# Other orders for the mixer's side steps, norm weights and bias row on VectorE, and a first stage that multiplies two column blocks together

## The reference

```
h = h + 1/2 * SwiGLU_a(RMSNorm(h))                    # d_ff 2816
u = RMSNorm(h) @ W_in                                 # width 3088: GLA q,k,v,gate,low rank; MoBA q,k,v
o = concat(GLA heads (4), MoBA heads (8)) @ W_out
h = h + o
h = h + 1/2 * SwiGLU_b(RMSNorm(h))
h = h + sigmoid(RMSNorm(h) @ W_pg) * (p @ W_pp)
out = RMSNorm(h)
```

## Time and profile before

| | us |
|---|---|
| median of the runs | 524.34 |
| the profiled execution | 523.98 |
| its span (first to last record) | 522.1 |
| TensorE matmul busy | 509.0 |
| VectorE busy | 328.8 |
| ScalarE busy | 277.0 |
| granted TensorE clock, mean | 0.996 |

### The profile page before, as it was taken

One profiled execution on the slowest core, in us unless ns is written; L12 is line 12 of the kernel. 1 busy time (PEld: TensorE's weight loads), 2 busy tenths in 40 slices (PEclk: granted clock), 3 DMA queues, 4 the chain that ended last, 5 costly groups with the idle time before them and its releaser, 6 DMA issues.

```text
span 522.1 us, 6951 instructions
## 1 busy us (share of the span) xinstructions
PE 509.0 (97%) x2499; PEld 413.9 (79%) x2499; DVE 328.8 (63%) x424; ACT 277.0 (53%) x352; POOL 97.0 (19%) x179
## 2 busy tenths in 40 slices
PE   8999999999999999999988999999999999999994
PEld 5778888888788888887776788888888888888883
DVE  4686556665636465699774885655656555473675
ACT  4974454444535276855674675345453452542836
POOL 1404232223210110220331000223222232120000
PEclk9999999999999999999999999999999999999998
DMA  8999888786787865754689385778778768648202
GB/s 255 369 312 340 269 245 254 210 243 214 237 262 266 263 219 207 241 163 125 211 281 249 126 298 171 256 243 257 222 229 255 236 229 240 219 136 273 75 0 80
DMA packets 79991, 117.20 MB, mean 224 GB/s; under 512 B 5952, under 2 KB 51984, under 8 KB 79840
## 3 DMA queue, kind: packets, MB, share of 16 engines
q1 hardware_dynamic: 71472, 93.34, 57.1%
q0 software_dynamic: 8336, 23.49, 13.4%
q10 hardware_dynamic: 160, 0.07, 0.0%
HBM read 106.12 MB, written 12.33 MB: 227 GB/s over the span
## 4 chain that ended last, share of the span: by engine, by line
PE 83%; DMA 5%; DVE 3%; ACT 3%; issue 2%; SPq 2%; POOL 1%; DVEq 0%; ACTq 0%; POOLq 0%
PE acc L568 81%; DMA pr_dram<-pr_sq 3%; SPq L431 1%; DMA prT<-pr_dram 1%; PE side L568 1%; DMA raw<-in_ffn_w_gu 1%; DVE w_lo L1243 1%; POOL prT L517 1%; PE turn L608 1%; ACT junk L938 1%; DVE gg L1530 0%; ACT w_hi L927 0%; PE turn L568 0%; DVE pr_sq L1507 0%; DVE AT L1553 0%
## 5 line engine op out<-in xcount | busy, mean ns | idle before, releaser
L1243 DVE TENSOR_TENSOR w_lo<-raw,w_hi 128x2048 fp32r<-128x2048 f32 (+1 forms) x87 | 192.6, 2216 | 98.1 <-ACT w_hi L927 97.9
L927 ACT ACTIVATE w_hi<-raw 128x2048 fp32r<-128x2048 f32 (+1 forms) x87 | 161.0, 1856 | 103.8 <-PE acc L568 103.7
L568 PE MATMUL acc<-w_hi,hT_hi 128*128 128x512 f32 x496 | 195.2, 393 | 0.5 <-DVE w_lo L1243 0.2
L568 PE MATMUL acc<-w_hi,hT_lo 128*128 128x512 f32 x496 | 193.2, 389 | 0.0
L568 PE MATMUL acc<-w_lo,hT_hi 128*128 128x512 f32 x496 | 193.1, 389 | 0.0
L568 PEld LDWEIGHTS acc<-w_hi,hT_hi 128*128 128x128 f32 x496 | 93.1, 188 | 22.0 <-issue 1.2
L568 PEld LDWEIGHTS acc<-w_hi,hT_lo 128*128 128x128 f32 x496 | 93.1, 188 | 19.7
L568 PEld LDWEIGHTS acc<-w_lo,hT_hi 128*128 128x128 f32 x496 | 93.2, 188 | 18.9
L479 POOL DMA_DIRECT2D act_in<-act_dram x92 | 50.1, 551 | 119.8 <-DMA act_dram<-act_sq 112.7
L568 PE MATMUL acc<-w_hi,a_hiT 128*128 128x512 f32 x176 | 68.6, 390 | 0.0
L568 PE MATMUL acc<-w_lo,a_hiT 128*128 128x512 f32 x176 | 68.5, 389 | 0.0
(11 more groups left out here) (178 smaller groups left out, 324.3 us busy)
## 6 DMA issues: line engine op xcount, KB each, us to landing
raw<-in_ffn_w_gu SPq DMA_DIRECT2D x82, 512.0 KB, 5.0
raw<-in_ffn_w_down SPq DMA_DIRECT2D x40, 512.0 KB, 5.3
raw<-in_w_in SPq DMA_DIRECT2D x24, 512.0 KB, 4.6
act_dram<-act_sq POOLq DMA_DIRECT2D x23, 256.0 KB, 5.5
act_in<-act_dram POOLq DMA_DIRECT2D x92, 64.0 KB, 3.6
raw<-in_w_out SPq DMA_DIRECT2D x8, 512.0 KB, 5.3
raw<-in_w_ple_gate SPq DMA_DIRECT2D x8, 512.0 KB, 5.5
raw<-in_ffn_w_gu SPq DMA_DIRECT2D x10, 256.0 KB, 6.1
```

The costliest lines, as they stand in the source:

```text
L568: return nc.tensor.matmul(o, lhsT, rhs, start=start, stop=stop, skip_group_check=True)
L927: A(w_hi[:, slot, :nk * N], raw[:, slot, :nk * N], ACT.Copy).then_inc(hi_ready, 1)
L1243: V.tensor_tensor(w_lo[:, slot, :nk * N], raw[:, slot, :nk * N], w_hi[:, slot, :nk * N].bitcast(F32), ALU.subtract).then_inc(lo_ready, 1)
```

## The change

1. First stage. The first four units become chunk pairs: unit u holds chunks 2u and 2u+1 of blocks 0 and 1 side by side. TensorE computes both blocks chunk by chunk (`first_pair`), so 12 matmuls per chunk of x, and for units 2 and 3 block 0 ahead of block 1. The pieces are five; units 2 and 3 are loaded and split whole. The order of ScalarE and VectorE: chunk 0 of x, pieces 0 and 1, chunk 1, piece 2, chunks 2 and 3, pieces 3 and 4, chunks 4 to 7, unit 2, then the squares, the root, unit 3. The first Silu comes behind the splits of units 4 and 5. The table loaded at the start is that of Sqrt instead of Silu.
2. Norm weights and bias row. TensorE's two steps go; `small_rows` does both on VectorE with two 32x32-square transposes, four copies, a memset and nine copies of bucket values. GpSimd sets two small tiles to zero and issues two DMAs less.
3. Mixer. `MIX`, `ACT_STEPS` and `DVE_STEPS` are reordered; no step is added or removed.

```diff
 MIX = {
     (35, 0): ["lr"],
     (35, 1): ["z"],
-    (37, 0): ["T_a"],
-    (38, 3): ["lv0"],
-    (40, 1): ["T_k0", "T_k1", "lv1"],
-    (40, 3): ["sc0.0", "sc0.1"],
-    (41, 0): ["lv2"],
-    (41, 2): ["sc1.0", "sc1.1"],
-    (42, 2): ["sc2.0", "sc2.1", "lv3"],
-    (43, 2): ["sc3.0", "sc3.1", "pv0"],
-    (44, 3): ["pv1"],
-    (45, 1): ["pvg0"],
-    (45, 3): ["pvg1", "pv2"],
+    (38, 0): ["T_a"],
+    (40, 1): ["T_k0", "T_k1"],
+    (40, 3): ["sc0.0", "sc0.1", "lv0"],
+    (41, 0): ["sc1.0", "sc1.1"],
+    (41, 3): ["sc2.0", "sc2.1", "lv1"],
+    (42, 2): ["lv2", "sc3.0", "sc3.1"],
+    (43, 3): ["lv3"],
+    (44, 1): ["pv0"],
+    (44, 2): ["pv1"],
+    (45, 1): ["pvg0", "pvg1"],
+    (45, 3): ["pv2"],
     (46, 1): ["pv3"],
-    (47, 2): ["T_o0"],
+    (47, 0): ["T_o0"],
     (47, 3): ["T_o1"],
 }
-ACT_STEPS = ["hi38", "tabE", "nat0", "z", "hi39", "T_a", "dg", "T_g0", "T_g1", "hi40", "nat1", "hi41", "hi42", "nat2", "T_q", "T_k0", "T_k1",
-             "hi43", "sc0", "nm0", "hi44", "sc1", "nm1", "nat3", "hi45", "sc2", "nm2", "hi46", "sc3", "nm3", "nat4", "pv0", "pv1", "hi47", "pvg", "pv2", "hi48", "pv3",
-             "nat5", "groot", "hi49"]
+ACT_STEPS = ["tabE", "hi38", "nat0", "z", "hi39", "hi40", "nat1", "hi41", "dg", "T_g0", "T_g1", "T_a", "hi42", "nat2", "T_k0",
+             "T_k1", "T_q", "hi43", "hi44", "sc0", "nm0", "sc1", "nm1", "hi45", "sc2", "nat3", "nm2", "hi46", "hi47", "sc3", "pv0",
+             "nm3", "nat4", "pv1", "hi48", "pvg", "nat5", "pv2", "groot", "pv3", "hi49"]
-DVE_STEPS = ["lr", "z", "g_sq", "zmin", "lo38", "la", "dot", "lo39", "Z0", "q_sq", "lv0", "lo40", "Z1", "Z2", "lo41", "lv1",
-             "sc0", "lv2", "lo42", "rc0", "Z3", "pr0", "sc1", "lo43", "rc1", "pr1", "sc2", "lv3", "lo44", "rc2", "pr2", "lo45", "sc3", "rc3", "pr3", "pv0", "lo46", "pv1", "lo47", "pvg", "pv2", "lo48", "pv3",
-             "gg", "o_g", "lo49"]
-PIECES = [(0, 0, 1), (0, 1, 1), (0, 2, 2), (1, 0, 2), (1, 2, 2), (2, 0, 2), (2, 2, 2)]
+DVE_STEPS = ["lr", "z", "g_sq", "dot", "lo38", "zmin", "lo39", "la", "q_sq", "lo40", "lo41", "Z0", "Z1", "lo42", "Z2", "sc0", "lv0",
+             "rc0", "sc1", "pr0", "lo43", "rc1", "sc2", "lv1", "pr1", "Z3", "lv2", "rc2", "lo44", "pr2", "sc3", "lv3", "rc3", "lo45",
+             "pv0", "pr3", "pv1", "lo46", "lo47", "lo48", "pvg", "pv2", "gg", "pv3", "o_g", "lo49"]
+PIECES = [(0, 0, 0, 1), (0, 0, 1, 2), (0, 1, 0, 2), (1, 0, 0, 2), (1, 1, 0, 2)]
...
             x_cols(0, 0, 2 * P)
             piece(0)
-            x_cols(1, 2 * P, N)
             piece(1)
             piece(2)
+            x_cols(1, 2 * P, N)
+            piece(3)
+            piece(4)
             x_cols(2, N, D)
-            for i in range(3, len(PIECES)):
-                piece(i)
+            pair_unit(2)
+            pair_unit(3)
...
+            def pair_part(u, k, b):
+                c = 2 * u + k
+                if b == 0:
+                    pe.wait_ge(turn_read, turned(f"h0.{c // 4}", c % 4 // 2) - 1 + c % 2)
+                if u < 2 and k == 0:
+                    pe.wait_ge(piece_lo, u + 1 + (b if u == 0 else 1))
+                else:
+                    pe.wait_ge(lo_ready, u + 1)
...
+            def first_pair():
+                pair_part(0, 0, 0)
+                pair_part(0, 0, 1)
+                h_turns(0, 0, [1])
+                pair_part(0, 1, 0)
+                pair_part(0, 1, 1).then_inc(unit_done, 1)
+                pair_part(1, 0, 0)
+                pair_part(1, 0, 1)
+                h_turns(0, 1)
+                pair_part(1, 1, 0)
+                pair_part(1, 1, 1).then_inc(unit_done, 1)
+                pair_part(2, 0, 0)
+                pair_part(2, 1, 0)
+                pair_part(3, 0, 0)
+                pair_part(3, 1, 0).then_inc(block0_done, 1)
+                pair_part(2, 0, 1)
+                pair_part(2, 1, 1).then_inc(unit_done, 1)
+                pair_part(3, 0, 1)
+                pair_part(3, 1, 1).then_inc(unit_done, 1)
...
-                        if f == 0 and n == 0 and k == 1:
-                            pe.wait_ge(bank_set, 1)
-                            o = side_open("gain")
-                            pe.wait_ge(gains_in, 48)
-                            flip(o[:, 0:3 * KC], gain_rows[:], 3 * KC).then_inc(side_done, 1)
-                            o = side_open("bias_row")
-                            pe.wait_ge(bias_in, 48)
-                            mm(o[0:MH, 0:BIAS_W], rel[:], rows[:], True, True).then_inc(side_done, 1)
...
-            for a in range(2):
-                h_turns(0, 0, [a])
-                keep_warm(4)
+            h_turns(0, 0, [0])
+            keep_warm(5)
...
-                    gated(f, b, j % 2)
                     if f == 0 and j == 0:
                         sp_(0)
-                    sp_(1)
+                        sp_(1)
+                        gated(f, b, j % 2)
+                    else:
+                        gated(f, b, j % 2)
+                        sp_(1)
...
-            A(spare[:, 0:1], spare[:, 1:2], ACT.Silu)
+            A(spare[:, 0:1], spare[:, 1:2], ACT.Sqrt)
...
+            def small_rows():
+                dve.wait_ge(gains_in, 48)
+                V.transpose(gain_sq[:], gain_rows[:]).then_inc(small_turned, 1)
+                dve.wait_ge(bias_in, 16)
+                V.transpose(relT[:], rel[:]).then_inc(small_turned, 1)
+                dve.wait_ge(small_turned, 1)
+                for j in range(4):
+                    V.tensor_copy(gains[32 * j:32 * j + 32, KC:], gain_sq[:, 32 * j:32 * j + 3 * KC]).then_inc(gains_set, 1)
+                V.memset(bias_row[:, T:], -1e30).then_inc(bias_set, 1)
+                dve.wait_ge(small_turned, 2)
+                half = BUCKETS // 2
+                V.tensor_copy(bias_row[:, T - half:T], view(relT[0:MH, :], [[-1, half]], half - 1)).then_inc(bias_set, 1)
+                for b, lo, hi in bucket_runs()[half:]:
+                    V.tensor_copy(bias_row[:, T - hi:T - lo], view(relT[0:MH, :], [[0, hi - lo]], b)).then_inc(bias_set, 1)
+                dve.wait_ge(gains_set, 4)
...
-            h_turns(0, 0, [0])
+            h_turns(0, 0, [0], [0])
             piece(0)
             piece(1)
+            h_turns(0, 0, [0], [1])
+            piece(2)
             h_turns(0, 0, [1])
-            piece(2)
-            h_turns(0, 1, [0])
             piece(3)
-            h_turns(0, 1, [1])
             piece(4)
-            piece(5)
-            piece(6)
+            h_turns(0, 1)
+            split(2)
             squares(0, 0)
             squares(0, 1)
             root(0)
```

More of the change, by code:

```diff
@@ L137, in plan_side @@
 def plan_side():
-    uses = ["gain0", "gain", "bias_row"]
+    uses = ["gain0"]
     for at in sorted(MIX):
@@ L156, in turned, with bucket_runs @@
     return TURN_AT[TURN[name] + k][1]
+def bucket_runs():
+    import math
+    import numpy as np
+    dist = np.arange(T)
+    nf = np.maximum(dist, 1).astype(np.float32)
+    exact = BUCKETS // 2
+    large = exact + (np.log(nf / np.float32(exact)) / np.float32(math.log(4096 / exact))
+                     * np.float32(BUCKETS - exact)).astype(np.int32)
+    bucket = np.where(dist < exact, dist, np.minimum(large, BUCKETS - 1))
+    runs, lo = [], 0
+    for d in range(1, T + 1):
+        if d == T or bucket[d] != bucket[lo]:
+            runs.append((int(bucket[lo]), lo, d))
+            lo = d
+    return runs
 def view(ap, dims, offset=0):
@@ L230, in build @@
         gain_rows0 = at("gain_rows0", 55, [KC, P])
[L231 to L234, removed]
+        gain_rows = at("gain_rows", 56, [32, P])
+        gain_sq = at("gain_sq", 57, [32, P])
+        rel = at("rel", 58, [BUCKETS, 32])
+        relT = at("relT", 59, [32, BUCKETS])
         bias_row = at("bias_row", 62, [MH, BIAS_W])
@@ L578, in unit @@
                 ks = ks or range(nk)
-                if ks[0] == 0 and not (isinstance(u, int) and u < 3):
+                if ks[0] == 0:
                     pe.wait_ge(lo_ready, u + 1)
@@ L629, in h_ready @@
                     pe.wait_ge(turn_read, turned(f"h{s}.{n}", a))
-            def piece_ready(i):
-                u, k0, nk = PIECES[i]
-                if k0 + nk == CH:
-                    pe.wait_ge(lo_ready, u + 1)
[L635 to L648, removed]
+            def pair_part(u, k, b):
[5 more added lines that the diff above has]
+                else:
+                    pe.wait_ge(lo_ready, u + 1)
+                hi, lo = [a[:, u, 2 * N * k:2 * N * (k + 1)].rearrange("p (g f) -> p g f", g=2)[:, :, b * FB:(b + 1) * FB]
+                          for a in (w_hi, w_lo)]
+                for m in range(M):
+                    l_hi, l_lo = from_hT(c, m)
+                    ins = exact3(acc[:, 2 * b + m, :].rearrange("p (g f) -> p g f", g=2), l_hi, l_lo, hi, lo, c == 0, c == KC - 1)
+                return ins
@@ L664, in gu_block @@
                     h_ready(s, 1)
-                elif f == 0 and isinstance(b, int) and b == 1:
-                    for i in (5, 6):
```

(33 more changed lines are left out.)

79 lines of the change are left out of this document (47 added, 32 removed).

## The result

The changed kernel takes 527.6 us, the median of 18 runs (525.1 to 532.03), against 523.67 for the kernel before, run beside it (18 runs). The ratio is 1.0077, with an interval of 1.0056 to 1.0097: slower by 0.8%, about 4 us. The forecast was 524.3, no change, with a range up to 526.7, so the time lies 0.9 above the range. Two executions in all the series ran at a granted clock of 0.65 and 0.56 throughout (before: 734.49 us; `e9_fill_all`: 869.63 us, the one that was profiled) and are left out everywhere, and the slowest run of `e7_both_late` (528.4) is left out of its ratio.

A forecast was written before the change was run, and what follows sets the result against it. TensorE's matmul chain was taken to set the time, so moments without matmul starts count. On the profiled execution, 523.98 - 1.1 + 4.7 - 3.6 = 523.98; with 0.36 to the median, 524.3 us, no change, range 522.3 to 526.7.

The forecast's parts named there:

- norm weights and bias row: First down projection, units 23 to 24: TensorE's gap goes, -1.1 us; VectorE's extra 2 to 4 us stays hidden.
- the first stage: First four weight units: unit 4 starts at 36.9 instead of 32.2, +4.7 us, bounds 4.0 and 5.5.
- Both waits: First stage: TensorE waits 2.7 us for unit 2's w_lo, until 23.2, and 2.7 for unit 3's, until 28.6.
- Rival D: First stage: waits for units 2 and 3 don't come, start and unit 3 gain, 518.5 us; chance 0.07.
- The lost table load: ScalarE ahead of unit 3's split: the 1.28 us load is gone, leaving about 0.5 for sum and root.
- the mixer's term, -3.6: Mixer: of 5.0 us of TensorE waits 1.4 remain, so -3.6 us, bounds -5.0 and -2.0.
- I take the middle of the two, 1.4 us of wait left: Mixer, pv3: midway between pair 3's data in time and 2.7 us late, the latter with a 6.06 us way out.
- rival B: Mixer: all DRAM trips take their longest, pv3 3 us late and pv1 1.3, 527.2 us; chance 0.08.
- the scores of pair 0: Mixer: a step given slack; pairs 0 to 2 keep over 2 us, so TensorE should not wait there.
- rival A, the clock: First stage: clock falls in the waits; absorbed in the first, +2.3 us in the second, 526.6; chance 0.15.
- the prediction's own signs of being wrong: Gaps missing or below 2 us, clock below 1.00 from 20 to 35 us, or waits for T_o0, T_a, pair 0's scores.
- the anchor: Whole kernel: terms added to the profiled execution's 523.98 us, then 0.36 added for the median, giving 524.3.

The follow-up runs named there:

- e9_fill_all: The changed kernel with 10 unused matmuls ahead of unit 2 and of unit 3, and 8 ahead of pv3: 525.90 us, ratio 1.0052 to the kernel before.
- e7_both_late: The changed kernel with unit 3 split ahead of squares and root, and unit 2 ahead of the copies of chunks 4 to 7: 522.21 us, ratio 0.9981.
- e12: The kernel before with the new first stage alone, unit 2 split ahead of chunks 4 to 7 and unit 3 ahead of the squares: 524.45 us, ratio 1.0019.
- e2: The kernel before with only the mixer's new orders: 522.30 us, ratio 0.9988 to the kernel before.
- e4: The changed kernel without its first stage (mixer orders, norm weights and bias row only): 521.10 us, ratio 0.9971 to the kernel before.
- e5: The changed kernel with 10 unused matmuls ahead of unit 2 and again ahead of unit 3: 528.14 us, ratio 1.0090 to the kernel before.
- e6: The changed kernel with unit 3 split ahead of the squares and root on ScalarE and VectorE: 524.69 us, ratio 1.0030 to the kernel before.
- e14: The changed kernel with the first stage's two waits filled with 10 unused matmuls each, repeated on another chip: 526.15 us, ratio 1.0062 to the kernel before.
- e8: The changed kernel without its first stage, with 8 unused matmuls ahead of pv3: 521.11 us, ratio 0.9965 to the kernel before.
- e13: The changed kernel itself, unchanged, run again as base of four kernels on one chip: 529.01 us, ratio 1.0110 to the kernel before.
- e1: The kernel before with only the new first stage: 530.08 us, ratio 1.0112 to the kernel before.
- e15: The changed kernel with 8 unused matmuls ahead of pv3 only: 526.20 us, ratio 1.0062 to the kernel before.
- e11: The changed kernel itself, unchanged, run again on another chip: 527.0 us, ratio 1.0081 to the kernel before.
- e10: The changed kernel with units 2 and 3 both split earlier and 8 unused matmuls ahead of pv3: 521.25 us, ratio 0.9953 to the kernel before.

## Why the prediction was wrong

**Right: norm weights and bias row.** -1.1 expected, -1.1 measured in each profile. VectorE's part took 2.1 us (estimated 2 to 4) and was hidden.

**Right in mechanism and nearly in size: the first stage.** Both waits came where they were laid out: until 23.4 (expected 23.2; the terms listed add up to 23.1) and until 28.9 (28.6; they add up to 28.45), by the chain that the prediction gives, turns of chunks 4 to 7 behind 36 matmuls and unit 2 queued behind them on ScalarE, then unit 3 behind the squares. Unit 4 was expected at 36.9 and came at 37.13, in the mean of three profiles at 37.7. The first matmul came 0.45 us earlier than expected (7.00 for 7.45), which the wait for a piece's `w_lo` at 11.38 took back (1.0 for 0.4). e7 and e12, which undo just these two places in the queues, show that this chain is the cause. Rival D (no waits) is refuted by every profile of this stage as it stands. The lost table load was worth less than its 1.28 us: from the end of the last square to unit 3's split it took 1.42 us before (20.86 to 22.28) and 0.54 after (23.89 to 24.43), since VectorE's sum, which ScalarE now waits for, ran under the load before. The prediction's 0.5 for sum and root has this right. The Trainium skill (ScalarE: Activation LUTs, What ACT_TABLE_LOAD costs) counts a drain of 1.38 us on top of the load. This case's trace does not agree: the load begins at 20.87, lasts 1.28 us, and the next instruction begins at 22.17.

**Wrong: the mixer's term, -3.6.** The step that failed is "I take the middle of the two, 1.4 us of wait left". The pair did leave on time (267.27 in e2, 266.6 expected). But its way out through DRAM took 5.8 to 6.5 us in all thirteen profiles with the new orders and 2.4 us in all four with the old ones: the long value of the earlier trace rows, which the prediction had as the bound and for which it named a likely reason, three weight units loading in these 10 us. In e2 the data came at 282.1, and the prediction gives 282.1 for that bound (e2 is 0.5 us late by then, so on the old scale it is 281.6). So rival B's place, at this pair, is the normal case: in the nine profiles without the mixer's filling TensorE starts `pv3` 1.7 to 3.0 us late, where 1.4 were taken. Second, the slack of the scores of pair 0, one of the steps it called safe, is gone: TensorE waits for q in ten of the thirteen profiles, 0.2 to 2.8 us. Third, the prediction priced a fall of the clock in the first stage alone; in the mixer it stood at nothing. The clock fell at `pv3` in four of those nine profiles (e4, e5, e6, e14) and at the wait for q in two of the thirteen (e8, e13). From `pv3` to unit 50 it took 28.2 us without a fall (e2, e7 and the changed kernel's first profile) and 29.7 to 31.1 with one. Together the mixer gains 0.6 us in the mean of the profiles (2.9 in the best, 3.3 lost in the worst) instead of 3.6: 1.9 where the clock holds, and a loss of 0.9 where it falls. That is 3.0 of the 3.3 us by which the forecast missed; the first stage adds 0.7 (5.4 for 4.7), the time outside the span, which the prediction left out, 0.3, and the kernel before, 0.7 lower beside the changed one than in the three runs shown first, takes 0.7 off. How much of the mixer's miss is the long way out and how much the wait for q is not separated.

**Wrong in chance: rival A, the clock, 0.15.** In each of the six profiles with a bare first wait (the changed kernel three times, e1, e6, e15) the clock fell in the first stage. It fell in the first wait in four and in the second in two (e1, e13). The split the prediction gave holds: in the first it is absorbed (unit 4 at 37.1 and 37.2; at 37.8 in e11; in e6 there is no second wait to absorb it), in the second it costs 1.0 to 1.4 us, less than the 2.3 expected, since seven or eight matmuls are slow and not ten. Two of the prediction's own signs of being wrong came with it: a clock below 1.00 between 20 and 35 us, and a wait for the scores of pair 0.

**Wrong in method: the anchor.** The sum was made against one profiled execution and carried over to the median with +0.36. For a kernel with a few waits behind which the clock sometimes falls, one execution does not stand for the median: the changed kernel's own profiled execution is 525.10, 2.5 below its median. Its runs range over 7 us, e10's, without such waits, over 2. That one execution lies 0.8 from the forecast, and this is luck: its mixer is the second shortest of the thirteen, and the clock held in it.

**What stays open.** Why e5 gained nothing while the same kernel gained 2.8 us against e13 on another chip (the intervals 1.0062 to 1.0119 and 1.0039 to 1.0085 overlap, e13 was high, and in the profiles of both e5 and e14 the clock fell at `pv3` instead), and why the two fillings don't add. What makes the way out long was never changed alone. The wait for q differs from execution to execution by up to 2.8 us, and no kernel here held it fixed. Time outside the span also moves (2.1 or 2.2 us in e13, 2.5 to 3.2 in e14), and no view shows what lies in it.

## What to carry to other kernels

When work is moved in one engine's order, go through what is queued behind it on each of the other in-order engines: here 24 matmuls put ahead of eight turns made ScalarE, then VectorE, then TensorE late twice, and moving two splits back recovered 5.0 us. A bare wait of 2 to 3 us on TensorE should be priced with its length plus the slow matmuls that may follow it. Filling it with matmuls on data that nobody reads held the clock in each filled place; what that gains in time is small and not settled here. Price a DMA round trip by its slow value when the new place lies beside the weight loads, and don't anchor on a single profiled execution where runs of one kernel differ by more than the effect.

## What the runs showed of the hardware that was not expected

- In the changed kernel's first profile the granted clock went from 1.00 to 0.50 (from the 2.4 to the 1.2 GHz level) behind a stretch of 2.7 us in which TensorE was idle (the wait for unit 2), and seven matmuls were slow. In e11 it fell about 2.1 us into the same wait. In e1 and e13 that wait left it at 1.00 and the next one, of 2.4 to 2.5 us, did not. In e5, with matmuls in the waits, it held through the first stage. In the kernel before, a wait of 1.6 us left it at 1.00.
- A write of 32x32 squares to DRAM (pair 3) took 2.4 us to its completion in the four profiles with the old orders and 5.8 to 6.5 in the thirteen with the new ones, and the whole trip, from the issue of the write to the use of the data, 11.2 to 11.9 against 14.3 to 15.8, with the same bytes.
